# One fp32 kernel, three edits: key and value projections by seven half products, two row maxima moved, the recurrence tail's VectorE work in a new order

## The reference, cut to what matters

```python
def hybrid_layer(x, ctx, ...):                     # x, ctx: [256, 1024]
    h  = rms_norm(x, norm_g) * (1 + scale) + shift
    hc = rms_norm(ctx, norm_g) * (1 + scale_c) + shift_c
    u_sh, g_rw, u_mla, g_mla = split(h @ w_in)     # w_in: [1024, 3488]
    uc_sh, gc_rw, uc_mla, gc_mla = split(hc @ w_in)
    # recurrence, 8 heads of 64, forward and backward:
    #   S = S * w_t + (S @ a_t) b_t + v_t k_t;  y_t = S @ r_t
    rw_c, states = rwkv_branch(prep(uc_sh), 0, ...)
    rw_l, _ = rwkv_branch(prep(u_sh), states, ...) # (norm(y_f + y_b) + bonus) * silu(g_rw)
    # attention, 8 heads, over 512 keys of x and ctx:
    mla_l = softmax_attend(q, k_all, v_all) * silu(g_mla)
    return x + gate * (concat(rw_l, mla_l) @ w_out)
# then a final rms_norm, and two layers of: S5 SSM, gated MLP over
# windows, differential attention, w_out; conv-gated MLP (w_up, w_down)
```

## Time and profile before

| what | us |
|---|---|
| runs | 1128.92, 1125.03, 1128.56 |
| median | 1128.56 |
| the profiled execution's own time | 1121.17 |
| its span | 1119.4 |

### The profile page before, as it was taken

One profiled execution on the slowest core, in us unless ns is written; L12 is line 12 of the kernel. 1 busy time (PEld: TensorE's weight loads), 2 busy tenths in 40 slices (PEclk: granted clock), 3 DMA queues, 4 the chain that ended last, 5 costly groups with the idle time before them and its releaser, 6 DMA issues.

```text
span 1119.4 us, 17999 instructions
## 1 busy us (share of the span) xinstructions
PE 1063.4 (95%) x7147; PEld 765.1 (68%) x7147; DVE 685.8 (61%) x1456; ACT 396.8 (35%) x1000; POOL 341.4 (30%) x246
## 2 busy tenths in 40 slices
PE   4999999998897897999999999999999999999998
PEld 2544858766786585647559999844656469999743
DVE  3222315586998985697536555698696356555755
ACT  2212213675654141634223444310535114444200
POOL 0000100220021011162027888600251037888400
PEclk9999999998898898999999999999999999999999
DMA  9922342000002302734237544533642244554430
GB/s 354 317 76 76 136 150 80 1 1 1 2 2 86 114 23 76 259 117 151 76 101 231 168 152 163 210 117 112 226 143 83 76 151 151 165 188 176 153 111 37
DMA packets 96981, 140.22 MB, mean 125 GB/s; under 512 B 12255, under 2 KB 63106, under 8 KB 96770
## 3 DMA queue, kind: packets, MB, share of 16 engines
q1 hardware_dynamic: 96532, 138.94, 36.5%
q10 hardware_dynamic: 366, 0.13, 0.0%
HBM read 138.01 MB, written 1.05 MB: 124 GB/s over the span
## 4 chain that ended last, share of the span: by engine, by line
PE 79%; DVE 13%; ACT 3%; DMA 2%; issue 2%; SPq 0%; POOL 0%; DVEq 0%; ACTq 0%
PE bank L1420 22%; PE bank L1460 12%; PE bank L883 10%; PE bank L1231 8%; PE bank L1222 3%; PE bank L499 2%; PE bank L492 2%; DMA ring<-in_ada_w 2%; PE bank L1092 1%; PE bank L1265 1%; PE bank L1163 1%; PE bank L556 1%; PE bank L509 1%; DVE ring L2367 1%; PE bank L680 1%
## 5 line engine op out<-in xcount | busy, mean ns | idle before, releaser
L3089 POOL TENSOR_TENSOR small<-small,con 128x8 f32<-128x8 f32 (+4 forms) x23 | 32.5, 1418 | 423.1 <-DVE small L2741 130.7
L883 PE MATMUL bank<-work,ring 128*128 128x256 f32 (+1 forms) x368 | 118.4, 479 | 0.0
L883 PEld LDWEIGHTS bank<-work,ring 128*128 128x128 f32 x368 | 70.0, 193 | 44.0 <-issue 38.5
L2970 DVE SCALAR_TENSOR_TENSOR bank<-work,prm,bank 128x256 f32<-128x256 f32 x176 | 76.8, 482 | 1.1 <-ACT bank L2030 1.0
L1231 PE MATMUL bank<-ring,work 128*128 128x512 f32 (+1 forms) x192 | 71.7, 526 | 0.0
L2014 ACT ACTIVATE work<-bank 128x128 f32<-128x128 f32 x120 | 33.2, 276 | 103.2 <-PE bank L1420 100.6
L1420 PE MATMUL bank<-xc,work 128*128 128x128 f32 x512 | 65.9, 275 | 2.0 <-ACT work L2014 2.0
L1420 PE MATMUL bank<-work 128*128 128x128 f32 x512 | 65.7, 275 | 0.0
L1420 PEld LDWEIGHTS bank<-xc,work 128*128 128x128 f32 x512 | 61.5, 192 | 2.5 <-ACT work L2014 2.4
L1420 PEld LDWEIGHTS bank<-work 128*128 128x128 f32 x512 | 61.4, 192 | 0.0
L1420 PE MATMUL bank<-work,ring 128*128 128x128 f32 x448 | 59.2, 275 | 0.0
(11 more groups left out here) (526 smaller groups left out, 2291.3 us busy)
## 6 DMA issues: line engine op xcount, KB each, us to landing
ring<-in_w_up SPq DMA_DIRECT2D x32, 1024.0 KB, 7.7
ring<-in_w_in SPq DMA_DIRECT2D x24, 1024.0 KB, 9.1
ring<-in_w_down SPq DMA_DIRECT2D x16, 1024.0 KB, 6.1
ring<-in_ada_w SPq DMA_DIRECT2D x12, 1024.0 KB, 10.5
work<-in_w_up SPq DMA_DIRECT2D x12, 1024.0 KB, 7.0
ring<-in_w_out SPq DMA_DIRECT2D x10, 1024.0 KB, 7.4
work<-in_w_in SPq DMA_DIRECT2D x4, 1024.0 KB, 9.2
work<-in_w_down SPq DMA_DIRECT2D x4, 1024.0 KB, 6.2
```

Source lines behind the costliest of these rows:

```text
L883: ins = mm(b[0:rows, 0:toks], wt[:, k, off:off + rows], hT[:, k, 0:toks], start=(k == 0), stop=(k == KD - 1))
L2970: ins = STT(out=c, in0=hp[:, m % 2, half, tap:tap + SEQ], scalar=k2(l, "conv01", 1, 44 * tap + FB * half + m), in1=c, op0=MUL, op1=ADD)
L3089: return G.tensor_tensor(out_, in_, C("negpow", 1, rows).to_broadcast([rows, n]), POW)
```

## The change

Three parts, which share no data.

1. **k and v.** Tiles 1 and 2 no longer go through `project`. Four pairs of blocks (two of k, two of v) are each made by seven products of 4 matmuls 128x256 (`mix_product`): half of the 1024 input channels, one block's 128 channels, half of the 512 tokens. GpSimd makes four weight sums 128x512 per pair, one of them in the ring slot itself. VectorE makes four sums of `hT` quarters 128x1024 once (`mix_in`), and per pair adds copies into PSUM (`upper_block` 128x512, `corner_block` 128x256). ScalarE makes three copies 128x256 per pair (`mix_part`). TensorE waits on four new semaphores: `mix_inputs` once, `mix_weights` once per pair, `mix_copies` three times per pair, `mix_corner` once per pair. Product 4 of a pair comes behind product 2 of the next; that of the last pair behind the first block of tile 3.
2. **Row maxima.** `row_maximum(0)` goes ahead of the STREAM_TRANSPOSEs of `turn_blocks(3)`, `row_maximum(1)` right behind them; each of the other 14 takes the place of the one before it.
3. **Tail.** VectorE first makes the bonus and gate products, takes over four copies 64x512 of `first` banks from ScalarE, then `add_cross`, the carries, reads and states without second-model work between them but `sine_angles(0, 0)`. `state_inputs`, `state_sums` and `state_maps` go behind the mix and ahead of the first output block's take; `rotation_tables` behind the first, `mixing_scalars` behind the second. On TensorE `spread_rstd(0)` goes right behind `spread_rstd(1)`, out of the output loop.

```diff
+        key_pairs = [(kind, p) for kind in "kv" for p in range(2)]
+        mix_in = take_work(A0, 4, KD // 2, SEQ)
+        mix_copy = take_work(A0 + 4096, 3, SEQ)
+        early_xc = xc[:, :, :].rearrange("p t n -> p (t n)")
+        mix_sum = {"k": take_work(26504, 3, 2, KD // 2, P),
+                   "v": early_xc[:, 0:3072].rearrange("p (q a k n) -> p q a k n", q=3, a=2, k=KD // 2)}
+
+        def mix_quarters(wt, p):
+            upper, lower = (wt[:, :, P * c:P * c + P] for c in (2 * p, 2 * p + 1))
+            return upper[:, 0:KD // 2], upper[:, KD // 2:KD], lower[:, 0:KD // 2], lower[:, KD // 2:KD]
...
-            for n in range(1, 4):
-                blocks = PROJ[n]
-                wt = weights(("in", n), KD, 512)
-                for i, block in enumerate(blocks):
-                    project(wt, block)
-                    if n == 3 and i in (1, 2):
-                        key_lengths((2 * i - 2, 2 * i - 1))
-                weights_done(blocks[-1][0:2])
+            mix_w = {}
+
+            def mix_product(q, i, first=False):
+                kind, p = key_pairs[q]
+                quarter, sums = mix_quarters(mix_w[kind], p), mix_sum[kind]
+                left = {1: quarter[0], 2: quarter[1], 3: sums[:, 2, p], 4: quarter[3], 5: sums[:, 0, p], 6: sums[:, 1, p], 7: quarter[2]}[i]
+                low, high = hT[:, 0:KD // 2, :], hT[:, KD // 2:KD, :]
+                right = {1: low[:, :, 0:SEQ], 2: high[:, :, 0:SEQ], 3: high[:, :, SEQ:512], 4: mix_in[:, 3], 5: mix_in[:, 0], 6: mix_in[:, 1], 7: mix_in[:, 2]}[i]
+                at = SEQ if i in (5, 3) else 0
+                b = bank_of((kind, 2 * p) if i in (2, 3, 5) else (kind, 2 * p + 1))
+                for k in range(KD // 2):
+                    ins = mm(b[:, at:at + SEQ], left[:, k, :], right[:, k, :], start=(first and k == 0), stop=(k == KD // 2 - 1), skip_group_check=True)
+                return ins
+
+            def mix_last(q):
+                kind, p = key_pairs[q]
+                pe.wait_ge(S["mix_corner"], q + 1)
+                mix_product(q, 4).then_inc(*filling((kind, 2 * p + 1)))
+                if p:
+                    weights_done((kind, 3), name=("in", 1 if kind == "k" else 2))
+            for q, (kind, p) in enumerate(key_pairs):
+                if not p:
+                    mix_w[kind] = weights(("in", 1 if kind == "k" else 2), KD, 512)
+                pe.wait_ge(*turn((kind, 2 * p + 1)))
+                mix_product(q, 1, True).then_inc(S["mix_products"], 1)
+                pe.wait_ge(*turn((kind, 2 * p)))
+                mix_product(q, 2, True)
+                if q:
+                    mix_last(q - 1)
+                else:
+                    pe.wait_ge(S["mix_inputs"], 1)
+                pe.wait_ge(S["mix_weights"], q + 1)
+                mix_product(q, 5).then_inc(S["mix_products"], 1)
+                pe.wait_ge(S["mix_copies"], 3 * q + 1)
+                mix_product(q, 6).then_inc(S["mix_products"], 1)
+                pe.wait_ge(S["mix_copies"], 3 * q + 2)
+                mix_product(q, 3).then_inc(S["mix_products"], 1)
+                pe.wait_ge(S["mix_copies"], 3 * q + 3)
+                mix_product(q, 7).then_inc(S["mix_products"], 1)
+            wt = weights(("in", 3), KD, 512)
+            for i, block in enumerate(PROJ[3]):
+                project(wt, block)
+                if not i:
+                    mix_last(3)
+                if i in (1, 2):
+                    key_lengths((2 * i - 2, 2 * i - 1))
+            weights_done(PROJ[3][-1][0:2])
...
@@ -1150,12 +1201,11 @@
             spread_gate(1)
             read_lengths(0)
             spread_rstd(1)
+            spread_rstd(0)
 
             wt_r = weights("out_recurrence", 4, 1024)
             for j in range(2):
                 for t in (1, 0):
-                    if not (j or t):
-                        spread_rstd(0)
...
+            def mix_part(q, n, part, lower, at):
+                kind, p = key_pairs[q]
+                act.wait_ge(S["mix_products"], 5 * q + n)
+                A.activation(mix_copy[:, part, :], bank_of((kind, 2 * p + lower))[:, at:at + SEQ], ACT.Copy).then_inc(S["mix_copies"], 1)
+
+            def copy_first(q):
+                mix_part(q, 1, 1, 1, 0)
+
+            def copy_rest(q):
+                mix_part(q, 2, 0, 0, SEQ)
+                mix_part(q, 3, 2, 1, 0)
...
+                        if kind in "kv":
+                            q = 2 * "kv".index(kind) + i // 2 + 1
+                            if q < 4:
+                                (copy_rest if i % 2 else copy_first)(q)
...
-            for stage in ("first", "last"):
-                for i in range(2, 4):
-                    for g in range(2):
-                        take_solved(stage, i, g)
+            for i in range(2, 4):
+                take_solved("first", i, 0)
+            for i in range(2, 4):
+                for g in range(2):
+                    take_solved("last", i, g)
...
+            TT(mix_in[:, 0], x12, x11, SUB).then_inc(S["vec_step"], 1)
+            TT(mix_in[:, 2], x22, x12, SUB)
+            vec.wait_ge(S["vec_step"], next(vec_steps))
+            TT(mix_in[:, 1], x22, mix_in[:, 0], SUB).then_inc(S["vec_step"], 1)
+            vec.wait_ge(S["vec_step"], next(vec_steps))
+            TT(mix_in[:, 3], x21, mix_in[:, 1], SUB).then_inc(S["mix_inputs"], 1)
+
+            def upper_block(q):
+                kind, p = key_pairs[q]
+                vec.wait_ge(S["mix_products"], 5 * q + 4)
+                vec.wait_ge(S["mix_copies"], 3 * q + 3)
+                b = bank_of((kind, 2 * p))
+                TT(b[:, :], b[:, :], mix_copy[:, 1:3, :].rearrange("p a n -> p (a n)"), ADD).then_inc(*filling((kind, 2 * p)))
+
+            def corner_block(q):
+                kind, p = key_pairs[q]
+                vec.wait_ge(S["mix_products"], 5 * q + 5)
+                b = bank_of((kind, 2 * p + 1))
+                TT(b[:, SEQ:512], b[:, 0:SEQ], mix_copy[:, 0, :], ADD).then_inc(S["mix_corner"], 1)
...
+                        if kind in "kv" and i % 2 == 0:
+                            upper_block(2 * "kv".index(kind) + i // 2)
+                            corner_block(2 * "kv".index(kind) + i // 2)
...
+                if n == 3:
+                    row_maximum(0)
                 turn_blocks(n)
+                if n == 3:
+                    row_maximum(1)
                 if n == 1:
                     for t in range(2):
                         vec.wait_ge(*when_empty(("q", t, 1)))
@@ -2470,9 +2569,9 @@
                         vec.wait_ge(S["q_tok"], t + 1)
 
             def maxima_between(step):
-                at = (3, 4, 8, 10, 12, 14, 16, 18, 21, 23, 24, 26, 28, 30, 34, 37)
+                at = (4, 8, 10, 12, 14, 16, 18, 21, 23, 24, 26, 28, 30, 34)
                 if step in at:
-                    row_maximum(at.index(step))
+                    row_maximum(2 + at.index(step))
...
-            state_inputs(0)
-            for i in range(2, 4):
-                for g in range(2):
-                    add_cross(i, g)
-            state_sums(0)
-            take_carry(4)
-            take_carry(5)
-            state_maps(0)
-            take_read(4)
-            take_read(5)
+            for j in range(2):
+                vec.wait_ge(*when_empty(("bonus", j)))
             for k in range(RB):
                 ins = STT(out=bon[:, k, :], in0=bon[:, k, :], scalar=col("lnx_b", 1, k), in1=grw[:, k, :], op0=ADD, op1=MUL)
             ins.then_inc(S["vec_step"], 1)
+            for i in range(2, 4):
+                key = ("first", i, 1)
+                vec.wait_ge(*when_full(key))
+                for d in range(2):
+                    rows = slice(64 * d, 64 * d + 64)
+                    ins = TC(factor(2 * i + d)[rows, 4:8, :].rearrange("p a b -> p (a b)"), bank_of(key)[rows, :])
+                ins.then_inc(*emptying(key))
             vec.wait_ge(S["vec_step"], next(vec_steps))
             for k in range(RB):
                 ins = TS(grw[:, k, :], grw[:, k, :], col("lnx_g", 1, k), 0.5, MUL, MUL)
             ins.then_inc(S["vec_step"], 1)
             vec.wait_ge(S["vec_step"], next(vec_steps))
+            for i in range(2, 4):
+                for g in range(2):
+                    add_cross(i, g)
+            take_carry(4)
+            take_carry(5)
+            take_read(4)
+            take_read(5)
             take_state(4)
+            take_state(5)
             sine_angles(0, 0)
-            take_state(5)
-            sine_angles(0, 1)
             take_read(6)
-            rotation_tables(0)
-            mixing_scalars(0)
             take_read(7)
...
+            sine_angles(0, 1)
...
+            state_inputs(0)
+            state_sums(0)
+            state_maps(0)
...
+                    if not j and t:
+                        rotation_tables(0)
+                    elif not j:
+                        mixing_scalars(0)
...
```

(17 more changed lines are left out.)

8 lines of the change are left out of this document (added).

## The result

| what | before | after |
|---|---|---|
| median of the first runs, us | 1126.88 (4 runs) | 1111.98 (4 runs, 1110.47 to 1114.29) |
| the profiled execution's own time, us | 1121.17 | 1110.47 |
| its span, us | 1119.4 | 1108.5 |
| ratio, 95% interval | | 0.9872 [0.9844, 0.9899] |

The change makes the kernel 1.3% faster, by 14.9 us of the medians. The two profiled executions differ by 10.9 us of span. So two things have to be explained: 1.7 us between the 9.2 of my sum and the 10.9 of the traces, and some 4 us between the traces and the medians.

The account below looks back on a forecast made before the run. TensorE bounds the key and value projections, VectorE the stretch behind the scores, both in turn the tail. Terms 6.5 + 4.8 + 0.1 - 2.2 = 9.2 us off the median 1128.56 gave 1119.4, range 1113.0 to 1126.0.

Parts of the forecast that it names:

- my sum: All terms over the whole kernel: 6.5 + 4.8 + 0.1 - 2.2 = 9.2 us faster.
- the last step, from the trace to the median: Whole kernel: profiled 1121.17 us lies 7.4 under the median 1128.56; gain taken off the median, giving 1119.4.
- part 3 forward: Tail up to the last output take: a TensorE wait is swapped for a VectorE backlog, gain 0.1 us.
- Part 1, 6.5 us: Key and value projections: 28 products take 48.4 us in place of 54.9, gain 6.5 us.
- D: Key and value products: GpSimd's first weight sums blocked by VectorE, 3.3 us late, total 1122.7; chance 0.08.
- E: Key and value products: GpSimd's slower sums become the bound, 38 us, total 1157.8; chance 0.04.
- Part 2, 4.8 us: Score stage: earlier maxima shorten TensorE's wait, the clock stays up, the reciprocal starts 4.8 us earlier.
- F: Behind the scores: the score stage's lead is lost as VectorE waits for TensorE; gain 4.4, total 1124.2; chance 0.07.
- Part 3 behind, -2.2 us: Behind the tail's output blocks: TensorE's new waits bring half clock, price 2.2 us.

Follow-up runs that it names:

- e2: Kernel before with only the key and value products changed to 28 half products: median 1120.12 us, ratio 0.9950.
- e9: The kernel before, unedited, profiled once more for a second look at its tail: 1127.88 us, median 1126.98.
- e3: Kernel before with only the row maxima moved: median 1123.74 us, ratio 0.9974.
- e10: The whole changed kernel again, unedited, run beside a later version: 1113.18 us, ratio 0.9889.
- e1: The whole changed kernel once more, beside the kernel before on one chip: median 1112.43 us, ratio 0.9880.
- e8: Whole change, with the second model's preparations placed in VectorE's idle times of the tail: 1110.34 us, ratio 0.9855 of before.
- e11: As e8, but rotation_tables and mixing_scalars moved behind final_scales: 1106.34 us, ratio 0.9827 of before.
- e5: The whole change without its tail edits: 1118.74 us, ratio 0.9925 of before.
- e12: As e8, but rotation_tables ahead of take_carry(4) and mixing_scalars behind take_carry(5): its one execution took 1106.55 us.

## Why the prediction was wrong in size

Two terms failed. The larger is the last step, from the trace to the median: 7.4 us taken as a constant. Behind it stands a term that was put at nothing, the half clock behind the waits that part 3 removes. The smaller is part 3 forward, 0.1 us, which measured 1.5.

- **Part 1, 6.5 us: right.** 48.4 us for the 28 products, 6.48 of lead ahead of the score stage (249.05 to 242.57). GpSimd's sums, the copies and the corners cost nothing, so D and E did not come. What D fears was there: the first four sums took 1.5 to 2.1 us each, 7.1 in all for my 5.2. But GpSimd began them at 49.03, not at 52.3 to 55.6, and the four were done at 56.1, 3 us before the first product that waits for them (59.24). By medians the part gave 5.6 to 5.9, by the averages above 5.9.
- **Part 2, 4.8 us: right in mechanism, 4.25 in the pair of traces.** All of it is the half clock: where it does not come by itself (e2), the old order is as fast, 46.88. In the stage, counted without part 1's lead, the last score that VectorE waits for came at 275.2 (268.69 + 6.48) for my 274.5, and the 20.9 us behind it were right; my own numbers gave 4.9, not 4.8. I priced the half clock as certain; the four later traces with the old order took 50.22, 50.22, 51.42 and 46.88 us. By medians 2.3 to 3.4.
- **Between the stages 1.05 us** (98.41 to 97.36) was luck: with the same code this stretch took 97.14 to 99.57, and the whole change itself had 97.36 and 98.85. The lead was not lost there, so F did not come either.
- **Part 3 forward, 0.1 us: the failing term of the traces.** It was 1.48. I took the 2.95 us of the earlier trace rows for eight TENSOR_SCALARs as their price, and moved it on as a debt. One of them had taken 1.81 us, and seven 0.25 each; moved away from GpSimd's sum the eight took 1.39, 1.56 less. With that, `state_maps` took 1.9 us for the 3.6 that I had moved and the four takes 0.3 less than I had, while the mix was ready 0.6 us later than I had worked out (37.1 us behind join(1), for 36.6): together the error of 1.4.
- **Part 3 behind, -2.2 us: right.** 661.8 in all five traces with the old tail, 664.2 to 664.8 with part 3: 2.4 to 3.0.
- **The step to the median: the failing step for the measured time.** I took 7.4 us as a constant offset between the profiled execution and the median, and subtracted the gain of one trace. It was no offset. Before's profiled execution was an uncommonly short one: of the 60 later executions of before four were as short as its 1121.17 or shorter. It had the short form of the half clock in its tail; e9 had the long one, 5.3 us more, at the median's clock, and it is the old order's waits of 2.45 and 2.32 us that go before it. The change removes these waits, so its median gained what the trace of before could not show. Of the five traces with the old tail three had the long form (64.12, 64.55, 65.86 us), two the short (58.83, 58.80); the second of the short ones, e3, was again 5.8 us under its kernel's median.

In sums: the traces' 10.9 are my 9.2, less 0.55 (part 2) and 0.2 (behind the tail), plus 1.4 (part 3 forward) and 1.05 (between the stages). For the medians two executions near their own median tell more than the first pair: e9 (1127.88, median 1126.98) and the profiled one of e10 (1114.22, median 1113.18). Their spans are 13.9 us apart, as the medians are (13.8): 6.5 ahead of the scores, 3.2 in them, 0.2 up to join(1), 6.8 in the tail, less 2.8 behind it. Averages over all traces, old code against new, give 5.9 + 3.0 + 0 + 5.0 - 2.7 = 11.2, part by part 5.9, 3.0 and 2.3, where the parts alone gave 5.9, 2.3 and 2.0. If every old tail had the long form, the same sum would be 13.6, as e1 measured. So what stays open is how often it comes: three of five traces of four kernels are too few to tell. Why the whole gained more than its parts did alone (10.2), and the 14.9 of the first runs, stay open too; the interval of e1 is 2.1 us wide to one side.

I had read the earlier trace rows as "a wait of 2.45 us was followed by half clock", and used it only against the change, at its new waits. The same reading, used on the waits that it removes, was worth more: I gave part 3 no clock gain at all, and that is what its tail gained most.

## What to carry to other kernels

When an edit removes or adds waits of the engine whose clock can fall, price both sides, and compare the mean granted clock of the runs with that of the profiled execution: if the profiled one is clearly faster than the median, it is not a typical sample of the stretches that you are about to change. Work that is moved off a path comes back where it is put; fill the times in which the engine waits anyway (e8, e11) before you queue it in front of the next consumer. And look at the longest of a group, not at the mean: eight instructions in 2.95 us were seven of 0.25 and one that stood. Put every stretch of the program into the table, also those that no edit touches: the first one here varied by 3.4 us with the same code.

## What the runs showed of the hardware

All TENSOR_SCALARs of `state_maps` (columns: engine, operation, count, shortest, median, longest in ns, first and last start in us), of before and of the changed kernel:

```profile
L2575 DVE TENSOR_SCALAR work<-work,con x16: 243/251/1811, 412.8 to 753.7; 128x64 f32<-128x64 f32 x16
```

```profile
L2674 DVE TENSOR_SCALAR work<-work,con x16: 245/247/255, 429.0 to 742.8; 128x64 f32<-128x64 f32 x16
```

and GpSimd before:

```profile
410.88 3.69 POOL L3125 TENSOR_TENSOR work<-small,con 128x2048 f32<-128x2048 f32 x1 [61.98 <-PE bank L801]
```

412.82 + 1.81 = 414.63, and 410.88 + 3.69 = 414.57: the VectorE instruction ended when GpSimd's did. e3 and e9 had the same pair (1.81 us). In e2 and e5 the same GpSimd instruction began 0.24 us ahead of the last one of `state_sums` instead, a TENSOR_TENSOR with two SBUF inputs that takes 0.29 us elsewhere; in e2:

```profile
400.44 3.69 POOL L3235 TENSOR_TENSOR work<-small,con 128x2048 f32<-128x2048 f32 x1 [62.94 <-PE bank L813]
```

```profile
400.68 3.59 DVE L2661 TENSOR_TENSOR work<-work 128x128 f32<-128x128 f32 x1
```

So all five traces of the old tail have such a stand, of 1.6 or 3.3 us, and those with part 3 as it stands have none: VectorE then runs only instructions with a PSUM input beside it. The two TENSOR_TENSORs with a PSUM input at 411.14 and 412.47 of before took their usual 0.42 in the middle of it. So a VectorE TENSOR_SCALAR on SBUF data, and a TENSOR_TENSOR with two SBUF inputs (3.59 us for 0.29 in e2, 3.64 for 0.22 in e12), did not end until a GpSimd instruction that began before them had ended. The Trainium skill, page "SBUF — State Buffer", section "Who interferes with whom", has this as an exclusive lock on a shared port pair, which blocks and does not slow: it names a VectorE instruction with two SBUF inputs beside a GpSimd instruction that reads SBUF, and one in a 2-port perf mode, which `tensor_scalar` can enter. The traces agree with the blocking; in which mode the TENSOR_SCALAR ran no run shows. A start 0.06 us behind GpSimd's was enough.

TensorE's clock fell to the lower of its levels behind waits of 2 to 3 us, but not behind each: 2.9 us in the old score stage was followed by 0.50 in before, and by 1.00 in e2. And the same two waits of the old tail had two prices: 0.50 up to 432 and back at 1.00 by 433 in before, still 0.56 on average over 439 to 448 in e9. It also fell where TensorE did not wait at all, behind products of one column and of 64 rows (L931, L659, up to 186.9); in before:

```profile
186.00:190.00 4.00, 4.00 (x17) 3.24 (x16) 1.68 (x6) 3.82 (x12) 0.72 (x1) 0.60 0.70 260
```
